# Second block's mixers on one Trainium2 core: the gate product moved to the front of the projection, the gate chain and the attention's transposes moved into it, normalization done head by head

## The reference, cut to what matters

```python
proj = h @ w_in                                  # 1024 -> 7*512 + 4 + 4
dq, dk, dv, mq, mk, mv, mo, mi, mf = split(proj)
lam = exp(sum(lv[0]*lv[1])) - exp(sum(lv[2]*lv[3])) + lam_init
# first mixer: differential attention, 4 heads, 2 maps of width 64, values 128 wide
q, k = rotary(dq) * 64**-0.5, rotary(dk)
a = softmax(causal(q0 k0')) - lam * softmax(causal(q1 k1'))
y_da = rms_norm(a @ v, subln_g) * (1 - lam_init)   # per head
# second mixer: mLSTM, 4 heads of 128, with causal conv (4 taps) and silu on mq, mk
lf = log_sigmoid(mf + b);  cumulative sums of lf, running maximum of mi - cumsum
h = sum_s(w_ts * (q_t k_s) * v_s) / max(|den|, exp(-m))
y_ml = sigmoid(mo) * (h - mean(h)) * rsqrt(var(h) + eps) * norm_g   # per head
mixed = concat([y_da, y_ml]) @ w_out
```

## Time and profile before

| | |
|---|---|
| median of 3 runs | 3110.1 us (3107.08 to 3111.24) |
| the profiled execution's own time | 3105.6 us |
| its span | 3103.7 us |
| mean granted TensorE clock | 0.942 of full |
| TensorE matmuls busy over the span | 2733.0 us, 88% |
| VectorE, ScalarE, GpSimd busy | 66%, 43%, 23% |
| first matmul of the second projection | at 1866.4 us |
| first exponential of the first mixer | at 2074.1 us |
| start of the next stage (`mix_out`) | at 2232.4 us |

### The profile page before, as it was taken

How to read it: one execution, slowest core, us unless ns; L and a number is a source line. 1 busy time by engine, 2 the same in 40 slices (tenths; PEclk the granted TensorE clock), 3 DMA queues, 4 the chain that set the end, 5 groups by cost and what they waited for, 6 DMA issues and landing times. The chain is left out here.

```text
span 3103.7 us, 35897 instructions
## 1 busy us (share of the span) xinstructions
PE 2733.0 (88%) x12788; PEld 2206.1 (71%) x12788; DVE 2045.1 (66%) x3562; ACT 1331.7 (43%) x2046; POOL 728.7 (23%) x565
## 2 busy tenths in 40 slices
PE   4976879799969999999999968977689699999994
PEld 3434668557757899999999956755567588888883
DVE  4334547789957777777777755324433499989984
ACT  2112552216633333333333333343243388878873
POOL 1000023140023333334444414410121221122220
PEclk8978989899989999999999989989889799999997
DMA  7610011244579988888888941222121399999993
GB/s 253 243 58 17 1 56 55 74 140 162 217 290 325 327 286 292 290 285 303 313 298 309 315 141 55 82 71 73 67 84 61 148 335 392 376 373 372 365 357 137
DMA packets 266033, 651.63 MB, mean 210 GB/s; under 512 B 48284, under 2 KB 109468, under 8 KB 264604
## 3 DMA queue, kind: packets, MB, share of 16 engines
q1 hardware_dynamic: 219436, 507.12, 45.5%
q0 software_dynamic: 46448, 142.67, 13.7%
HBM read 617.09 MB, written 57.74 MB: 217 GB/s over the span
## 5 line engine op out<-in xcount | busy, mean ns | idle before, releaser
L2933 ACT ACTIVATE ex_w_hi<-expert_raw 128x1024 fp32r<-128x1024 f32 x384 | 377.0, 1071 | 49.5 <-DMA expert_raw<-in_w 26.9
L1760 PE MATMUL bank<-v_hi,peer_w_hi 128*128 128x512 f32 x768 | 301.5, 393 | 20.9 <-DVE peer_w_lo L1866 20.9
L212 POOL TENSOR_TENSOR w_lo<-ring,w_hi 128x512 fp32r<-128x512 f32 (+1 forms) x136 | 173.4, 1309 | 558.5 <-ACT w_hi L202 558.5
L2979 DVE TENSOR_TENSOR ex_w_lo<-expert_raw,ex_w_hi 128x1024 fp32r<-128x1024 f32 x256 | 296.7, 1219 | 9.2 <-ACT ex_w_hi L2933 7.8
L1760 PE MATMUL bank<-v_lo,peer_w_hi 128*128 128x512 f32 x768 | 301.3, 392 | 0.0
L1760 PE MATMUL bank<-v_hi,peer_w_lo 128*128 128x512 f32 x768 | 301.3, 392 | 0.0
L1802 ACT ACTIVATE v_hi<-v_in 128x1024 fp32r<-128x1024 f32 x128 | 130.6, 1056 | 329.3 <-PE bank L1760 302.1
L1735 POOL DMA_INDIRECT got_rows<-in_u_rows,diff x128 | 183.8, 1436 | 315.1 <-DVE got_rows L1834 287.5
L1748 PE MATMUL bank<-h_hi,u_hi 128*128 128x384 f32 x768 | 257.1, 335 | 0.3 <-DVE u_lo L1827 0.3
L1748 PE MATMUL bank<-h_hi,u_lo 128*128 128x384 f32 x768 | 257.2, 335 | 0.0
L1748 PE MATMUL bank<-h_lo,u_hi 128*128 128x384 f32 x768 | 256.9, 334 | 0.0
(11 more groups left out here) (498 smaller groups left out, 6138.4 us busy)
## 6 DMA issues: line engine op xcount, KB each, us to landing
expert_raw<-in_w SPq DMA_DIRECT2D x384, 512.0 KB, 8.6
v_in<-in_expert_v SPq DMA_DIRECT2D x128, 512.0 KB
u_in<-in_u_tiles SPq DMA_DIRECT2D x96, 512.0 KB
ada_in<-in_w_ada SPq DMA_DIRECT2D x48, 512.0 KB, 5.1
gates_by_key<-spread SPq DMA_DIRECT2D x6, 4096.0 KB, 11.8
gate_in<-gates_by_key SPq DMA_DIRECT2D x384, 64.0 KB
ring<-in_w_in SPq DMA_DIRECT2D x11, 2048.0 KB, 8.4
early_u<-in_u_tiles SPq DMA_DIRECT2D x32, 512.0 KB, 3.8
```

Source lines behind the costliest of these rows:

```text
L212: eng.tensor_tensor(g.w_lo[:, k, 0:cols], g.ring[u % RING][:, k, 0:cols], g.w_hi[:, k, 0:cols].bitcast(F32), ALU.subtract).then_inc(s["z_f ...
L1760: last = pe.matmul(g.bank[2 + o][:, :], x[:, par, e, i * P:(i + 1) * P], v[:, par, e, c], start=(first and n == 0), stop=(final and n == 3 ...
L2933: act.activation(hi[kind][:, c, :], raw_piece(raw, u * PIECES + c), ACT.Copy).then_inc(s["r_hi"], 1)
L2979: dve.tensor_tensor(lo[which][:, c, :], raw_piece(raw, u * PIECES + c), hi[which][:, c, :].bitcast(F32), ALU.subtract).then_inc(s["r_lo"], 1)
```

## The change

- **Gates first.** The gate columns become the first unit, one group with a stationary operand of eight columns, evicted to one tile of eight rows; SP copies the forget rows to a tile at partition 0. `Products` gets `shared=1`: VectorE's share of the splits is now of unit 1. In the plan the unit moves ahead of the seven wide ones.
- **Gate chain in the projection** (class `Gates`): logarithms on ScalarE after conv_in 1, scans on VectorE after convolution 3, Exp after conv_in 5, transposes on TensorE after the first dq group, evictions after dq tile 1. The selector is built by GpSimd behind its splits.
- **Flips in the projection.** Eight groups of four transposes follow eight of the last ten groups, into banks 6 and 7; Silus, Sigmoid of mo and the lambda chain move in too.
- **Head by head.** In `differential`, `squares(h)` and `weigh_head(h)` follow units 6, 10, 14; in `mlstm`, `center(h - 2)` follows the last tile of heads 2 and 3, with `close(h)` behind the loop. `sums(h - 1)` and `outs` move to tile 2 of head h.
- **Filler.** `MEMORY_FIRST` is 6. `differential` runs ten parts in its loop and two behind it; `mlstm` none at its start, 14 in its loop, six behind it (`LAST = 6`), two of whose three evictions come after the second Sqrt.

```diff
     def by_dve(self, n, k):
-        return n == 0 and k % 2 == 1
+        return n == self.shared and k % 2 == 1
+class Gates:
+    def sp(self, sp):
+        sp.wait_ge(self.s["l_small"], 1)
+        sp.dma_start(self.mf[:, :], self.both[ML_H:2 * ML_H, :]).then_inc(self.s["n_mf"], 16)
+    def act_logs(self, act):
+        act.wait_ge(s["n_mf"], 16)
+        act.activation(self.ex[:, :], self.mf[:, :], ACT.Abs).then_inc(s["n_abs"], 1)
+        act.wait_ge(s["n_abs"], 1)
+        act.activation(self.cum[:, :], self.ex[:, :], ACT.Exp, scale=-1.0).then_inc(s["n_exp"], 1)
+        act.wait_ge(s["n_exp"], 1)
+        act.activation(self.logs[:, :], self.cum[:, :], ACT.Ln, bias=self.g.ones[0:ML_H, 0:1]).then_inc(s["n_log"], 1)
...
 def project_second(...):
+            products = Products(g, ctx, s, first_unit, [(0, True, slice(0, 2 * ML_H), WHOLE)]
+                                + [(1 + n // 4, True, chunk(n % 4), WHOLE) for n in range(8)]
+                                + [(3 + n // TT, False, WHOLE, chunk(n % TT)) for n in range(5 * TT)], shared=1)
 ... SP
+                g.prefetch(sp, first_unit + 1 + RING)
+                gates.sp(sp)
                 g.prefetch(sp, first_unit + 8 + RING)
 ... TensorE
+                products.pe(pe, 0, g.bank[7][0:2 * ML_H, :])
                 for n in range(8 + 5 * TT):
+                    products.pe(pe, 1 + n, g.bank[n % 6][:, :])
+                    if n == 8:
+                        gates.pe(pe, g.bank[6])
+                    if n == FLIPS:
+                        pe.wait_ge(s["n_tc"], 2)
+                    if FLIPS <= n < FLIPS + 8:       # FLIPS = 18
+                        flip(n - FLIPS)
 ... ScalarE
                     act.activation(raw[:, c % 4, :], g.bank[n % 6][:, :], ACT.Copy).then_inc(s["l_raw"], 1)
+                    if c == 1:
+                        gates.act_logs(act)
+                    if c == 5:
+                        gates.act_floor(act)
...
+                        if u == 1 and i == 0:
+                            act.wait_ge(s["l_conv"], 4 * 8)
+                            for c in range(8):
+                                act.activation(conv[:, c, :], conv[:, c, :], ACT.Silu).then_inc(s["l_cdone"], 1)
+                        if u == 4 and i == 1:
+                            act.wait_ge(s["l_tok"], 4 * TT)
+                            act.activation(mo, mo, ACT.Sigmoid).then_inc(s["l_gate"], 1)
+                            act.wait_ge(s["l_lam"], 1)
+                            act.activation(nlam[:, :], dots[:, :], ACT.Exp).then_inc(s["l_lexp"], 1)
 def differential(...):
+            FIRST_PART = N - 2 * (MEMORY_FIRST - 1)
...
+                for index in range(N - FIRST_PART, 2 * MEMORY_FIRST):
+                    mem.part(pe, index)
 ... VectorE
+                    if u >= TT + 2 and u % TT == 2:
+                        squares(u // TT - 1)
+                squares(DA_H - 1)
+                weigh_head(DA_H - 1)
 def mlstm(...):
+            def center(dve, step, h):
+                num, total = y[:, :, h, 0:ML_D], y[:, :, h, ML_D:ML_D + 1].rearrange("p i o -> p (i o)")
+                dve.wait_ge(s["n_y"], 2 * h + 2)
...
+                step(dve.tensor_tensor(num, num, neg[:, :, h].unsqueeze(2).to_broadcast(wide), ALU.mult))
+                step(dve.tensor_reduce(mu[:, :, h], num, AX_X, ALU.add))
+                step(dve.tensor_scalar(mu[:, :, h], mu[:, :, h], 1.0 / ML_D, None, ALU.mult))
+                step(dve.tensor_tensor(num, num, mu[:, :, h].unsqueeze(2).to_broadcast(wide), ALU.subtract))
+                step(dve.tensor_tensor(sq[:, :, :], num, num, ALU.mult))
+                dve.tensor_reduce(var[:, :, h], sq[:, :, :], AX_X, ALU.add).then_inc(s["n_sq"], 1)
+                step(dve.tensor_tensor(mo[:, :, at], mo[:, :, at], gain[:, at].unsqueeze(1).to_broadcast(wide), ALU.mult))
 ... VectorE
                         if n:
                             weigh(dve, n - 1)
+                        if j == 3 and h >= 2:
+                            center(dve, step, h - 2)
                 weigh(dve, ML_H * TT - 1)
+                center(dve, step, ML_H - 2)
+                for h in range(ML_H - 1):
+                    close(dve, step, h)      # reciprocal, product with it, product with mo
+                center(dve, step, ML_H - 1)
+                close(dve, step, ML_H - 1)
 ... ScalarE
                 outs(act, ML_H - 1)
+                roots(0, ML_H - 1)
+                mem.act(act, (PARTS - LAST) // 2)
+                roots(ML_H - 1, ML_H)
+                for j in range((PARTS - LAST) // 2 + 1, PARTS // 2):
+                    mem.act(act, j)
 ... TensorE
                 sums(ML_H - 1)
+                for index in range(PARTS - LAST, PARTS):
+                    mem.part(pe, index)
 def plan_weights(g):
+    g.plan(a["w_in_2"][0], W2_GATES, 2 * ML_H, 1)
     for c in (W2_MQ, W2_MK, W2_DQ, W2_DK, W2_DV, W2_MO, W2_MV):
         g.plan(a["w_in_2"][0], c, BANK)
-    g.plan(a["w_in_2"][0], W2_GATES, 2 * ML_H, 2)
-MEMORY_FIRST = 5
+MEMORY_FIRST = 6
```

More of the change, by code:

```diff
@@ L220, in dve @@
                 self.low(dve, 0, k)
+        for k in range(1, DC, 2) if self.shared else ():
+            self.low(dve, self.shared, k)
     def pool(self, pool):
@@ L1928, in project_second @@
         cbias = sb("conv_bias", [P, 8])
[L1929 to L1933, removed]
+        gbias = sb("gate_bias", [2 * ML_H, 1])
+        lv = sb("da_lv", [P, 4, RD])
+        prod = sb("da_prod", [P, 2, RD])
+        dots = sb("da_dots", [P, 2])
+        mo = tok[:, :, 3 * BANK:4 * BANK]
+        FLIPS = 8 + 2 * TT + 2
+        with stage(nc, "l_par l_raw l_conv l_cdone l_tok l_small l_ones l_dve l_rot l_flipped l_flip_out l_gate l_lam l_lexp" + Gates.SEMS + Products.SEMS) as (block, s):
+            gates.open(mo, s)
+            products = Products(g, ctx, s, first_unit, [(0, True, slice(0, 2 * ML_H), WHOLE)]
+                                + [(1 + n // 4, True, chunk(n % 4), WHOLE) for n in range(8)]
+                                + [(3 + n // TT, False, WHOLE, chunk(n % TT)) for n in range(5 * TT)], shared=1)
             @block.sync
@@ L1944, in _, with flip @@
                 pool.memset(mv[:, :, :, ML_D:ML_D + 1], 1.0).then_inc(s["l_ones"], 1)
+                gates.pool_ones(pool)
                 products.pool(pool)
+                gates.pool_select(pool)
             @block.tensor
             def _(pe):
+                def flip(n):
+                    x = tok[:, :, (n // 4) * BANK:(n // 4 + 1) * BANK]
+                    pe.wait_ge(s["l_rot"], n // 4 + 1)
+                    if n >= 2:
+                        pe.wait_ge(s["l_flip_out"], n - 1)
+                    for i in range(TT):
+                        last = pe.transpose(g.bank[6 + n % 2][:, i * P:(i + 1) * P], x[:, i, (n % 4) * P:(n % 4 + 1) * P], g.ident[:, :])
+                    last.then_inc(s["l_flipped"], 1)
+                products.pe(pe, 0, g.bank[7][0:2 * ML_H, :])
                 for n in range(8 + 5 * TT):
@@ L1954, in _, with flip_out @@
                         pe.wait_ge(s["l_tok"], n - 6 - 8 + 1)
-                    products.pe(pe, n, g.bank[n % 6][:, :])
-                for c in range(2):
-                    products.pe(pe, 8 + 5 * TT + c, g.bank[6 + c][0:ML_H, :])
+                    products.pe(pe, 1 + n, g.bank[n % 6][:, :])
[5 more added lines that the diff above has]
+                        flip(n - FLIPS)
             @block.scalar
             def _(act):
-                base = g.before(first_unit)
+                def flip_out(n):
+                    act.wait_ge(s["l_flipped"], n + 1)
+                    act.activation(g.ht[:, n, :], g.bank[6 + n % 2][:, :], ACT.Copy, scale=RD ** -0.5 if n < 4 else 1.0).then_inc(s["l_flip_out"], 1)
+                base = g.before(first_unit) + 1
                 products.act_start(act)
+                products.act_unit(act, 1)
+                act.wait_ge(s["l_par"], 64)
+                act.wait_ge(g.dense, base)
+                act.activation(gates.both[:, :], g.bank[7][0:2 * ML_H, :], ACT.Identity, bias=gbias[:, 0:1]).then_inc(s["l_small"], 1)
                 n = 0
@@ L2213, in sb @@
             return ctx.enter_context(nc.sbuf_tensor(name, shape, dt))
-        row = [sb(f"ml_row{n}", [ML_H, T]) for n in range(6)]
-        sel = sb("ml_sel", [ML_H, ML_H, P])
-        key_u = sb("ml_u", [P, TT, ML_H])
-        floor = sb("ml_floor", [P, TT, ML_H])
+        run, sel, key_u, floor = gates.run, gates.sel, gates.key_u, gates.floor
         gap = sb("ml_gap", [P, 2, T])
```

270 lines of the change are left out of this document (136 added, 134 removed).

## The result

The changed kernel takes 3070.87 us (median of 4 runs, 3060.13 to 3080.68) against 3109.82 us before (median of 4 runs): ratio 0.9885, 95% interval [0.9863, 0.9908], 39.0 us faster. Predicted were 3067.6 us, range 3055 to 3085. The profiled execution took 3070.07 us, span 3068.2 us.

The account below looks back on a forecast made before the run. Stages closed by barriers bound it: TensorE limits the loops, but for 74.6 us between them does not work on what comes next. Gains 21.4 + 4 + 17.1 = 42.5 us give 3063, plus 4.5 for timed runs 3067.6 us, range 3055 to 3085.

Parts of the forecast that it names:

- Entry: Second projection up to the first mixer's first exponential: 21.4 us gained, range 19 to 24.
- The head: Start of the second projection: putting the gate group first, at a low clock, loses 2.5 us.
- The wide unit's splits ... are ready before they are read: Projection head: splits shared with VectorE follow the gate group chunk by chunk, so TensorE does not wait for them.
- One sign of being wrong: Projection: the prediction is wrong if its wide groups take more than 5.45 us.
- First mixer: Loop and stretch behind it: 3.6 + 1 = 4.6 us gained, taken as 4, range 1 to 7.
- 1 us gained: First mixer's loop: following busy TensorE instead of a slow stretch, it gains 1 us, range 0 to 3.
- the first of the three inserted heads: First mixer's loop: three heads' passes on VectorE, 2.1 us each, cost 0, at most 6 us.
- Second mixer: Whole stage: start 11.2, loop 3.9 and tail 2.0 sum to 17.1 us gained, range 12 to 24.
- the cover is just enough: Second mixer's loop: TensorE's work covers centring two heads on VectorE, 5.2 us each; cost 0, at most 4 us.
- the 29.2 that I took: Second mixer's tail: stage ends 29.2 us after unit 14's scores, where the old needed 31.2; 2 us gained.
- VectorE's heads: Rival: inserted head passes delay TensorE in both mixers, 16.7 us if all shows, 3084; chance 0.17 for half or more.
- The clock did stay low: Rival: projection stays at 0.43 us a matmul after the gate product, all such groups giving about 3200; chance 0.02.

Follow-up runs that it names:

- E2: Changed kernel with all eight weight splits of the projection's first wide unit on VectorE, none on GpSimd; 3065.71 us, ratio 0.9865 to the kernel before.
- E3: Changed kernel with all four heads' squares, sums and gains behind the first mixer's loop, still head by head; 3067.66 us, ratio 0.9874 to the kernel before.
- E8: Changed kernel run once more, unchanged, on the same chip as three other runs; 3068.83 us.
- E4: Changed kernel with the centring of heads 0 and 1 moved behind the second mixer's loop; 3075.26 us, ratio 0.9908 to the kernel before.
- E1: Changed kernel with ScalarE evicting memory group 8 before the second root at the second mixer's end; 3067.94 us, ratio 0.9884 to the kernel before.

## Why the prediction was right

**Entry.** Predicted 21.4, measured 20.2 (the first exponential 188.5 us after the first matmul, for 187). The moves were right: Silu, Sigmoid, lambda and logarithms lie under the groups, and the scans delayed nobody. The head was off: 3.4 us lost instead of 2.5, and for another reason than mine; the gate group itself was quicker than I took it for. "The wide unit's splits ... are ready before they are read" was wrong; I priced VectorE's splits as if GpSimd did not touch them, though the trace before had two of 1.77 us. E2 shows that the loss goes with that collision. The flips inside cost some 0.5 us each, for the 0.6 reckoned. From the first wide eviction to the last it is 169.8 us for 165.2, so all inserted work shows as 4.7 us where 4.2 were reckoned. One sign of being wrong did appear: groups for mq and mk that follow each other within a unit are 5.60 us apart in all eleven traces, where they had been 5.45; I have no cause for it. The wait at the first unit change did not grow (from group 1 to group 4 20.9 us for 20.73).

**First mixer.** The tail is as worked out, 6.95 us for "about 7", bounded by the memory parts and their store. "1 us gained" by a warmer clock was the wrong term: the loop was 59.5 us, then 59.4, 59.5, 57.1, 57.8 and 59.1 in other traces with the same loop, against 58.6. The clock does rise on average (0.94 for 0.88; 0.79 for 0.65 in the first head), and yet that head took 15.9 us instead of 14.65. What counts is where the low stretch falls. Before, 10.2 us of it lay early in the head, where TensorE waits 3.6 us for VectorE even at full clock (E3), and cost about 1.5 us, an estimate from 14.65 against E3's 13.1. After, 6.8 us of it lay over the last 25 matmuls, which do not wait, and cost 2.8. So an average clock was the wrong measure for this term. Besides, the first of the three inserted heads costs 1.1 us where I said 0.

**Second mixer.** Predicted 17.1, measured 14.9 (16.5 in E8). Its start gained 10.8 for 11.2, the way to unit 14's scores 3.1 for 3.9: the first 8 us ran at a clock of 0.57, more than the 1.5 us I had taken off, and 0.97 us is one wait behind centre(0), where I said the cover is just enough (it is a wait for a memory eviction of ScalarE; in E4, without the centres inside, it is not there). The end came 30.2 us behind the scores of unit 14 and as described: parts 18 and 19 alone behind 5.3 us of idleness, 5.19 us long; E1 shows that order is the cause. Here the sum itself slipped: its terms, 21.2, then 5.4 to 7, then 2.8, make 29.4 to 31.0, and the 29.2 that I took lies below them. The three parts erred the same way, 4.6 us in sum (42.5 and 37.9), and the median came out 3.3 us above the forecast. That it came so near is in part luck, for four runs of the changed kernel lie 20 us apart.

**Rivals.** VectorE's heads show only 1.1 us in the first mixer (E3) and 1.7 us in the second (E4) of the 16.7 possible. The logarithms were in time. The clock did stay low for stretches, but no wide group of the projection after the first ran at 0.43 us.

## What to carry to other kernels

When work is moved into a loop, look at what stands behind a late wait on an in-order engine: one eviction queued behind a root cost 5.8 us, its reordering nothing. Before putting passes over all heads into a loop, try cutting them by head behind it: in E3 the engine that runs ahead did three of four while it would have waited, and the end came no later. Do not count on VectorE and GpSimd to split two tensors side by side: VectorE alone did eight in 4.90 us, the two sharing them stalled one for 5.23. And price a low clock by the matmuls that it falls on, not by the mean of a stretch.

## What the hardware did unexpectedly

A VectorE operation that takes 0.68 us alone took 5.23 us beside four successive GpSimd operations of 1.28 us, and much the same in four other traces; in a sixth it took 2.76. The same loop of the same program took 57.1 to 59.5 us from one execution to the next, 2.4 us of it from the granted clock in its first head (0.57 to 0.87), which is as much as the flips inside gained (2.0 to 2.5).
